# Hidden-tile reloads on SyncE's queue, single-pair down turns at the start, and a reordered first gate/up turn in a two-layer trunk kernel

## What is computed

```python
mod = c_act @ ada_w[l] + ada_b[l]
sh1, sc1, g1, sh2, sc2, g2 = split(mod, 6)
...
h = rms_norm(x, norm_ffn_g[l]) * (1 + sc2) + sh2
x = x + g2 * ((silu(h @ w_gate) * (h @ w_up)) @ w_down)
```

## Time and profile before

| | us |
|---|---|
| median of three runs | 2639.61 (2637.91 to 2639.83) |
| profiled execution, its own time | 2635.11 |
| its span | 2633.3 |
| TensorE busy | 2445.9 |
| VectorE busy | 1495.0 |
| GpSimd busy | 1127.5 |
| ACT busy | 822.3 |

### The profile page before, as it was taken

One profiled execution on the slowest core, in us unless ns is written; L12 is line 12 of the kernel. 1 busy time (PEld: TensorE's weight loads), 2 busy tenths in 40 slices (PEclk: granted clock), 3 DMA queues, 4 the chain that ended last, 5 costly groups with the idle time before them and its releaser, 6 DMA issues.

```text
span 2633.3 us, 31770 instructions
## 1 busy us (share of the span) xinstructions
PE 2445.9 (93%) x10858; PEld 1999.6 (76%) x10858; DVE 1495.0 (57%) x2270; ACT 822.3 (31%) x1479; POOL 1127.5 (43%) x1580
## 2 busy tenths in 40 slices
PE   6999999969999988787989999996979999998999
PEld 5788878858888867676768888874857888886887
DVE  6537776684455444444757777777485544543222
ACT  4102232233333320000346666663143333320001
POOL 3443335375666643333222222233166656644521
PEclk7999999989999998898989999997989999999999
DMA  7543447313423365555211111114213333255431
GB/s 280 168 128 99 134 132 268 96 56 113 128 90 111 120 248 186 182 185 180 91 37 33 33 40 32 32 45 146 79 60 110 111 113 125 91 208 192 172 116 64
DMA packets 262837, 318.02 MB, mean 121 GB/s; under 512 B 8331, under 2 KB 168229, under 8 KB 262565
## 3 DMA queue, kind: packets, MB, share of 16 engines
q1 hardware_dynamic: 220800, 209.74, 24.5%
q10 hardware_dynamic: 41892, 106.46, 11.3%
...
## 4 chain that ended last, share of the span: by engine, by line
PE 80%; DVE 9%; DMA 6%; issue 2%; ACT 2%; POOL 1%; ACTq 0%; SPq 0%; DVEq 0%; POOLq 0%
PE psG L820 21%; PE psG L825 21%; PE psG L826 21%; PE psZ L820 3%; PE psZ L826 3%; PE psZ L825 3%; DMA ada_raw<-in_ada_w 3%; DMA w_raw<-in_ffn_w_down 1%; PE psM L1215 1%; PE psG L1256 1%; PE psZ L1245 1%; DVE ada_acc L1917 1%; PE psO L820 1%; PE psO L825 1%; PE psO L826 1%
## 5 line engine op out<-in xcount | busy, mean ns | idle before, releaser
L799 POOL TENSOR_SCALAR w_split<-w_raw 128x256 fp32r<-128x256 f32 x448 | 194.1, 459 | 1018.9 <-PE psG L820 301.8
L726 POOL TENSOR_TENSOR f_w<-f_raw,f_w 128x256 fp32r<-128x256 f32 x528 | 455.4, 886 | 239.6 <-ACT f_w L1358 238.4
L820 PE MATMUL psG<-h_hi,w_split 128*128 128x512 f32 x1088 | 439.1, 404 | 21.7 <-DVE h_lo L1905 12.4
L825 PE MATMUL psG<-h_lo,w_split 128*128 128x512 f32 x1088 | 429.1, 394 | 0.0
L826 PE MATMUL psG<-h_hi,w_split 128*128 128x512 f32 x1088 | 428.6, 394 | 0.0
L803 POOL TENSOR_TENSOR w_split<-w_raw,w_split 128x256 fp32r<-128x256 f32 x448 | 354.6, 821 | 0.0
L820 PE MATMUL psG<-hid,w_split 128*128 128x512 f32 x704 | 282.4, 401 | 31.9 <-POOL w_split L803 20.8
L820 PE MATMUL psG<-h_hi,f_w 128*128 128x512 f32 x704 | 278.4, 395 | 17.5 <-DVE f_y L2418 16.8
L826 PE MATMUL psG<-hid,w_split 128*128 128x512 f32 x704 | 279.6, 397 | 0.0
L825 PE MATMUL psG<-hid,w_split 128*128 128x512 f32 x704 | 279.6, 397 | 0.0
L825 PE MATMUL psG<-h_lo,f_w 128*128 128x512 f32 x704 | 276.8, 393 | 0.0
...
## 6 DMA issues: line engine op xcount, KB each, us to landing
f_spill<-f_stg SPq DMA_DIRECT2D x88, 512.0 KB, 2.7
hid<-f_spill ACTq DMA_DIRECT2D x32, 1024.0 KB, 10.9
f_raw<-in_ffn_w_gate SPq DMA_DIRECT2D x44, 512.0 KB, 3.8
f_raw<-in_ffn_w_up SPq DMA_DIRECT2D x44, 512.0 KB, 4.3
w_raw<-in_ffn_w_down SPq DMA_DIRECT2D x44, 512.0 KB, 4.5
ada_raw<-in_ada_w SPq DMA_DIRECT2D x40, 512.0 KB, 4.3
ada_raw<-in_ada_w ACTq DMA_DIRECT2D x40, 512.0 KB, 3.8
w_raw<-in_ev_w_in SPq DMA_DIRECT2D x28, 512.0 KB, 3.8
```

The costliest lines, as they stand in the source:

```text
L726: lo = nc.gpsimd.tensor_tensor(slot[:, 1, parts[q]], src[:, parts[q]], slot[:, 0, parts[q]].bitcast(F32), ALU.subtract)
L799: nc.gpsimd.tensor_scalar(slot[:, 0, part], raw[:, part], 1.0, 1.0, ALU.mult, ALU.mult).then_inc(hi_done, 1)
L820: mm = nc.tensor.matmul(o, st[0], mv[0], start=first, stop=False, **kw)
L825: nc.tensor.matmul(o, st[0], mv[1], start=False, stop=False, **kw)
```

## The change

1. `DOWN_TURNS` takes pairs 0, 1 and 2 alone, then two at a time: seven turns, 112 steps in place of 96. `ADA_AT` and `ADA_COLS_AT` are spread anew, and a group's matmuls come two steps after its last part (one before).
2. All hidden reloads are in SP's program. Each waits for what frees its buffer (`HID_AFTER`: the end of a down turn) and stands ahead of the slab named in `HID_BEFORE`. ACT's queue keeps the `ada_raw` loads alone. `x_old` is read back in two halves, one before and one after the last spills.
3. Turn 0's order of products is 11, 21, 22, T2, T3, T1, T4 (22 into the free banks `psO` and `psM`), and from 22 on gate and up alternate by feature tile. Turns 1 to 10 keep their order.
4. T2 no longer starts from normalised blocks 12 and 11: ACT scales `xT` (tiles 0 to 3, second token half) by the gains, VectorE subtracts it from the scaled tiles 4 to 7, all before the root is known; then one multiplication by the root and one addition. T1 is made from 22 - T2. GpSimd makes the low parts of T2 and T1, VectorE those of T3 and T4. Eight weight sums move ahead of the projection's last step, the switch to the SiLU table later.
5. `newton` takes three operations.

```diff
+FIRST_TURN = ("p1", "p2", "p3", "p6", "p7", "p5", "p4")
+LATER_TURN = ("p1", "p2", "p6", "p7", "p5", "p3", "p4")
+FIRST_SUMS = {4: (0, 1, 2, 3), 5: (4, 5), 6: (6, 7)}
-DOWN_TURNS = [(0,), (1, 2), (3, 4), (5, 6), (7, 8), (9, 10)]
-HID_OF = {0: 0, 1: 2, 2: 3, 3: 0, 4: 1, 5: 2, 6: 3, 7: 0, 8: 1, 9: 2, 10: 3}
+DOWN_TURNS = [(0,), (1,), (2,), (3, 4), (5, 6), (7, 8), (9, 10)]
+HID_BEFORE = {2: (1,), 4: (2,), 6: (3, 4), 10: (5, 6), 14: (7, 8), 18: (9, 10)}
+HID_AFTER = {4: 0, 5: 1, 6: 2, 7: 3, 8: 3, 9: 4, 10: 4}
+HID_OF = {0: 0, 1: 2, 2: 3, 3: 1, 4: 0, 5: 2, 6: 3, 7: 1, 8: 0, 9: 2, 10: 3}
-ADA_AT = [16 + 8 * k // 5 for k in range(40)]
-ADA_COLS_AT = [ADA_AT[4 * g + 3] + 1 for g in range(10)]
+ADA_AT = [16 + 4 * k for k in range(8)] + [48 + 3 * k // 2 for k in range(32)]
+ADA_COLS_AT = [ADA_AT[4 * g + 3] + 2 for g in range(10)]
...
-            def hid_load(eng, l, pair):
+            def hid_load(l, pair):
                 for n in range(2):
-                    eng.wait_ge(fs_out[n], 32 * (f_turn(l, pair) + 1))
+                    sp.wait_ge(fs_out[n], 32 * (f_turn(l, pair) + 1))
+                if pair in HID_AFTER:
+                    sp.wait_ge(gemm_done, G(f"ffb{l}", 0, 16 * HID_AFTER[pair] + 15))
+                else:
+                    sp.wait_ge(fp_done, f_prod(l, PAIRS - 1, (1, 9, 11, 3)[pair]) + 1)
...
+            def x_again(l, h):
+                sp.wait_ge(fp_done, f_prod(l, PAIRS - 1, 5 if h else 7) + 1)
+                sp.wait_ge(fx_out, 48 * (l + 1))
+                sp.dma_start(x_old[:, 1 - h], x_dram.rearrange("k p t -> p k t")[:, :, half(h)]).then_inc(fx_back[h], 16)
...
                     for s in range(2, P_):
+                        for pair in HID_BEFORE.get(s, ()):
+                            hid_load(int(phase[-1]), pair)
                         slab_load(phase, 0, s)
...
-                for i in range(1, PAIRS):
+                for i in range(PAIRS):
                     for b in range(PRODUCTS):
                         f_block(l, i, b)
+                        if (i, b) in ((0, 11), (1, 1)):
+                            for k in range(4):
+                                t_low(l, "t1" if i else "t2", k)
...
+                for b in range(4, PRODUCTS, 2):
+                    begin(0, b)
+                    begin(0, b + 1)
+                    for k in range(4):
+                        operand_wait(OPERAND[f_order(0)[b // 2]], k)
+                        piece(0, b, k)
+                        piece(0, b + 1, k)
...
+            def ada_loads():
+                act.wait_ge(fp_done, f_prod(0, PAIRS, 0))
+                for k in range(40):
+                    ada_load(k)
...
-                    V.tensor_tensor(nt[:], nt[:], n_r[:], ALU.mult).then_inc(n_newt, 1)
-                    dve.wait_ge(n_newt, 3 * g + 1)
-                    V.tensor_scalar(nt[:], nt[:], -0.5, 1.5, ALU.mult, ALU.add).then_inc(n_newt, 1)
-                    dve.wait_ge(n_newt, 3 * g + 2)
-                    V.tensor_tensor(n_r[:], n_r[:], nt[:], ALU.mult).then_inc(n_newt, 1)
+                    V.scalar_tensor_tensor(nt[:], nt[:], -0.5, n_r[:], ALU.mult, ALU.mult).then_inc(n_newt, 1)
+                    dve.wait_ge(n_newt, 2 * g + 1)
+                    V.scalar_tensor_tensor(n_r[:], nt[:], 1.5, n_r[:], ALU.add, ALU.mult).then_inc(n_newt, 1)
...
-                    if (h, m) == (1, 6):
-                        for n in range(4):
+                    if h == 1 and m >= 4:
+                        difference(l, m - 4)
+                        for n in FIRST_SUMS.get(m, ()):
                             w_sum(l, 0, n)
                 norm.add(1, KT - 1)
-                for n in range(4, 8):
-                    w_sum(l, 0, n)
                 norm.newton(1)
...
+                def t2_sum(k):
+                    dve.wait_ge(ft_e, 8 * l + k + 1)
+                    V.tensor_tensor(f_t2[:, k], f_t2[:, k], n_r[:], ALU.mult).then_inc(ft_e, 1)
+                    dve.wait_ge(ft_e, 8 * l + 4 + k + 1)
+                    V.scalar_tensor_tensor(f_t2[:, k], n11[k], sh[4 + k], f_t2[:, k], ALU.add, ALU.add).then_inc(ft_sum, 1)
...
+            def difference(l, k):
+                dve.wait_ge(ft_u, 4 * l + k + 1)
+                bank_wait(dve, f"out{l}", 0, KT + 4 + k)
+                V.scalar_tensor_tensor(f_t2[:, k], xT[:, 4 + k, half(1)], modA[:, 2 * l + 1, 4 + k:5 + k], f_t2[:, k],
+                                       ALU.mult, ALU.subtract).then_inc(ft_e, 1)
```

More of the change, by code:

```diff
@@ L118 @@
     ("ffa0", 1, dict()),
-    ("ffb0", 1, dict(slab=22, step=96, misc=10, ada=40)),
+    ("ffb0", 1, dict(slab=22, step=112, misc=10, ada=40)),
     ("norm2", 1, dict(misc=2)),
@@ L127 @@
     ("ffa1", 1, dict()),
-    ("ffb1", 1, dict(slab=22, step=96)),
+    ("ffb1", 1, dict(slab=22, step=112)),
 ]
@@ L199, in build @@
         n_sum = at("n_sum", N0 + 4 * KB, [H])
-        n_r = at("n_r", N0 + 6 * KB, [H])
-        n_t = [at(f"n_t{n}", N0 + (8 + 2 * n) * KB, [H]) for n in range(2)]
+        n_t = [at(f"n_t{n}", N0 + (6 + 2 * n) * KB, [H]) for n in range(2)]
+        n_r = at("n_r", N0 + 10 * KB, [H])
         f_raw = at("f_raw", WO, [4, D])
@@ L369, in build @@
         fx_out = sem("fx_out")
-        fx_back = sem("fx_back")
+        fx_back = [sem(f"fx_back{h}") for h in range(NH)]
         fn_ht = sem("fn_ht")
@@ new lines, in begin @@
+                def begin(i, b):
+                    bank_free(i, f_order(i)[b // 2], b % 2)
+                    pe.wait_ge(fw_ready, f_prod(l, i, b) + 1)
+                for b in range(4):
+                    begin(0, b)
+                    for k in range(4):
+                        if b % 2 == 0:
+                            operand_wait(OPERAND[f_order(0)[b // 2]], k)
+                        piece(0, b, k)
+                    if b == 0:
+                        norm_pe(norm, 1)
+                for b in range(4, PRODUCTS, 2):
+                    begin(0, b)
+                    begin(0, b + 1)
+                    for k in range(4):
+                        operand_wait(OPERAND[f_order(0)[b // 2]], k)
+                        piece(0, b, k)
+                        piece(0, b + 1, k)
@@ L1154, in down @@
+                for i in range(1, PAIRS):
+                    for b in range(PRODUCTS):
+                        begin(i, b)
+                        for k in range(4):
+                            piece(i, b, k)
             def down(phase, next_norm=None):
@@ L1330, in _ @@
             down("ffb1")
-            for last_step in range(92, 96):
+            for last_step in range(108, 112):
                 bank_wait(pe, "ffb1", 0, last_step)
@@ L1880, in _ @@
             gate_up(1, x_wait("out1", lambda h, k: (0, 8 * h + k)))
-            down(1)
             for t in range(KT):
```

308 lines of the change are left out of this document (167 added, 141 removed).

## The result

The changed kernel takes 2554.27 us (median of 4 runs, 2553.06 to 2555.93); the kernel before, run beside it, 2638.96 us. The ratio is 0.968, 95% interval 0.9663 to 0.9696: 84.7 us less, where 96 were forecast. The profiled execution took 2554.76 us (span 2552.8), 80.35 us less than that of before.

The account below looks back on a forecast made before the run. TensorE, busy 93% of the span, was taken as the bound, so only its waits and slow-clock stretches could be won. 73 + 8 + 14 + 1 = 96 us off gave 2543 us against the median, range 2528 to 2575.

Parts of the forecast that it names:

- The modulation loads: Layer 0's down phase: ada_raw loads freed from waiting behind hidden reloads, 252 us against 325.4, -73 us.
- the opening's "3 us": Layer 0's down phase: the 3 us counted for its opening within the forecast 252 us.
- The opening: Start of the down phases: no wait for the second slab, pair 1 stalls 2 us, doubt 3; layer 1 -8 us.
- The sum of 5.2 MB: Layer 0's opening: spill, x_old, hidden and slab bytes behind the last spill, taking 16 us, landed near 987.
- The first gate/up turn: Turn 0 of gate/up in each layer: 62 us instead of 69.4, -7 us per layer, -14.
- The new wait: First gate/up turn: TensorE stands after its first product until the sum of squares ends, 4 to 5 us.
- the full rule: First turn: VectorE waits for GpSimd's whole instruction, 0.3 us more on some 25 operations, 7 us; sum 2557 us.
- Norm roots: Path to norm 2's tiles: one VectorE operation less, 0.5 us, twice, -1 us.
- The first (the turn gives nothing): Rival: the first gate/up turn gains nothing, 2557 us, bounds up to 2563; chance 0.15.
- The second (pair 1's tiles late by as much as the slab before): Rival: down phases' opening not improved, slab or pair 1's tiles as late as now, 2561 us; chance 0.05.
- The third: Rival: ada_raw loads still land late beside the bursts, 63 of the 73 us stay, 2606 us; chance 0.07.
- The fourth (SP's queue): Rival: gated reloads on SP's in-order queue delay the slabs of double down turns, 2783 us; chance 0.03.

Follow-up runs that it names:

- the queue alone: The kernel before with only the reloads of hidden pairs 3 to 10 moved to SP's queue: 2588.37 us against 2639.94, ratio 0.9803.
- the run with the other order: The changed kernel with second_y of m = 0 ahead of hidden(0,0) and hid_low(0,0) behind second_y of m = 1: 2557.16 us, ratio 0.9685.

## Why the prediction was right, and where it was not

**The modulation loads (73 forecast, 66.3 measured).** The mechanism is confirmed part by part: the queue alone gives 47 us, the loads still come a few us late, and the second step absorbs them. Most of the 7 us that are missing lie in the opening, not in the ada stalls (0.3 us in that phase). The term that was mis-sized is the opening's "3 us": it is 5.2 us at the stall, 2.3 of slow clock after it, and 1.2 at 1000.95, when VectorE was held up (below), 8.7 us in all.

**The opening (a stall of 2 to 3 forecast, 5.0 and 3.0 measured).** The early slab came as forecast: no wait. Pair 1's slab was split from 986.3, forecast 987 to land; that these agree is luck, two errors that cancel. From the last spill it took 18.2 us (968.1 to 986.3), not 16. The sum of 5.2 MB had left out two `ada_raw` loads, which the change itself lets start at 965.95; with these held back it still took 17.3 us, against 17.4 to 18.5 in six profiles with them, so they explain 1 us at most, and what the rest is stays open. In layer 1, which has none, it took 16.1 us, as summed. And the due time, 989.6, had been worked out from the old start of the phase, 967.8; the shorter first turn brought it to 963.7 + 21.8 = 985.5. The start of the wait was taken in the time of the kernel before, its end in that of the changed one. Layer 1's down phase gave 7.0 of 8.

**The first gate/up turn (7 us each forecast, 4.3 and 2.8 measured).** The new wait came nearly as forecast (4 to 5 us; 3.83), T2 started at 545.39 (forecast 545), ran into T3 with 0.6 us between them, T1's wait was 3.96 us (forecast some 4). The step that failed is the end: T4 began at 575.91 and turn 0 ended at 582.95, not at 579 to 580. T4's wait was 4.26 us where the sum had 3.5, since `hidden` and `hid_low` stand ahead of the products' sums on VectorE (1.4 us, as the run with the other order shows), T4's eight operations took 8.6 us, and the slow stretches after the waits cost 8.8 us instead of 6 to 7. In layer 1 the turn of before was 67.6 us and not the 69.1 of its row: behind its last wait the slow pace lasted 2.8 us instead of the 5.3 of layer 0, and 1.5 us of the forecast gain were never there to win.

The Trainium skill, SBUF — State Buffer, section "SBUF: two separate sides", calls the port pair that VectorE and GpSimd share an exclusive lock. The prediction counted 1.0 us for an operation of VectorE beside GpSimd; T2's eight took 9.1 us, 1.14 each. A wait for a whole half tile of GpSimd (0.86 us) behind the 0.69 us of the operation alone would be 1.55 us. That is 0.55 us more than 1.0 and not the 0.3 that the prediction gave to the full rule; the time measured is nearer to the count than to the rule.

**Norm roots (1 us).** Lost in the 2.7 us by which the stretch between the layers varies; neither shown nor refuted.

**The rivals.** The first (the turn gives nothing) did not come true, though the turns gave 7.1 us of 14. The second (pair 1's tiles late by as much as the slab before) came in part: 5.0 and 3.0 us, where the slab had cost 10.6 and 10.2. The third is refuted by the run with the queue alone. The Trainium skill, DMA: Bandwidth & Descriptors, section "Issuing engines are not separate DMA queues", says that starting DMAs on several engines saves only the time to issue them. By that alone this rival would have come true, and these runs do not bear it out: here 512 KB `ada_raw` loads land in 4.3 us at 1030 to 1060 while SP's `w_raw` loads behind the reloads take 9.0. The fourth (SP's queue) did not appear: after 1001 us TensorE has no wait for a slab or for hidden tiles in that phase.
